# Moving the convolution, the norms, the bias and the transposes of a four-branch mixer to other engines and places

## The reference

```python
h = _rmsnorm(x, g_mix[l])
gate_pre, a_in, na_qkv, dil_qkv, swa_q, swa_kv = jnp.split(h @ w_in[l], IN_SPLITS, axis=-1)
# branch a: a * sigmoid(g), depthwise convolution of 31 taps over the rows, layernorm, silu
# branch b: norm of q and k, softmax(q k / 8 + bias[head, row, key]) v over near keys (4 heads)
# branch c: norm and rope, three dilated windows; branch d: norm and rope, window of 128, sinks
gates = jax.nn.sigmoid(gate_pre.reshape(bsz, seq, N_BRANCH, D_MODEL) + gate_b[l])
x = x + jnp.sum(gates * jnp.einsum('bsnc,ncd->bsnd', ys, w_branch[l]), axis=2) @ w_out[l]
```

## Time and profile before

| | us |
|---|---|
| runs | 1758.84 and 1754.22; median 1758.84 |
| profiled execution | 1755.16 |
| its span | 1753.5 |
| first mixer in it | about 868 to 1117 |
| second mixer in it | about 1311 to 1558 |

### The profile page before, as it was taken

How to read it: one execution, slowest core, us unless ns; L and a number is a source line. 1 busy time by engine, 2 the same in 40 slices (tenths; PEclk the granted TensorE clock), 3 DMA queues, 4 the chain that set the end, 5 groups by cost and what they waited for, 6 DMA issues and landing times. The chain is left out here.

```text
span 1753.5 us, 26990 instructions
## 1 busy us (share of the span) xinstructions
PE 1657.0 (94%) x10967; PEld 1493.6 (85%) x10967; DVE 1137.5 (65%) x1635; ACT 833.2 (48%) x1253; POOL 459.3 (26%) x529
## 2 busy tenths in 40 slices
PE   7889899999999889999999998999999999899998
PEld 6767799987786778998888998899988899889997
DVE  5885565545556755665467966677646796767763
ACT  6445454434345454444453336556534433656552
POOL 2400100002330010000137933043303694314430
PEclk9999999999989999999999999999999999999999
DMA  7422366555231134765465342666546434367651
GB/s 263 160 77 90 106 169 193 183 201 197 77 123 47 36 112 127 201 179 192 137 223 166 122 145 96 173 190 192 185 136 214 162 127 139 104 177 202 177 186 71
DMA packets 293165, 265.58 MB, mean 151 GB/s; under 512 B 18609, under 2 KB 254129, under 8 KB 293041
## 3 DMA queue, kind: packets, MB, share of 16 engines
q1 hardware_dynamic: 293040, 263.85, 48.5%
HBM read 262.78 MB, written 1.05 MB: 150 GB/s over the span
## 5 line engine op out<-in xcount | busy, mean ns | idle before, releaser
L144 DVE TENSOR_TENSOR w_lo<-w_raw,w_hi 128x2048 fp32r<-128x2048 f32 (+1 forms) x246 | 566.2, 2304 | 301.0 <-ACT w_hi L143 295.2
L143 ACT ACTIVATE w_hi<-w_raw 128x2048 fp32r<-128x2048 f32 (+1 forms) x246 | 465.1, 1894 | 227.8 <-PE bank L470 126.4
L1766 PE MATMUL bank<-h_hi,w_hi 128*128 128x256 f32 x1984 | 567.0, 286 | 2.9 <-DVE h_lo L259 1.1
L1767 PE MATMUL bank<-h_lo,w_hi 128*128 128x256 f32 x1984 | 562.4, 283 | 0.0
L1768 PE MATMUL bank<-h_hi,w_lo 128*128 128x256 f32 x1984 | 562.2, 283 | 0.0
L1766 PEld LDWEIGHTS bank<-h_hi,w_hi 128*128 128x128 f32 x1984 | 381.8, 192 | 4.6 <-issue 4.4
L1767 PEld LDWEIGHTS bank<-h_lo,w_hi 128*128 128x128 f32 x1984 | 381.9, 193 | 0.3
L1768 PEld LDWEIGHTS bank<-h_hi,w_lo 128*128 128x128 f32 x1984 | 381.7, 192 | 0.0
L397 PE MATMUL bank<-w_hi,h_hi 128*128 128x512 f32 (+2 forms) x304 | 118.6, 390 | 7.6 <-DVE h_lo L259 3.7
L399 PE MATMUL bank<-w_hi,h_lo 128*128 128x512 f32 (+2 forms) x304 | 116.8, 384 | 0.0
L398 PE MATMUL bank<-w_lo,h_hi 128*128 128x512 f32 (+2 forms) x304 | 116.7, 384 | 0.0
(11 more groups left out here) (433 smaller groups left out, 2998.2 us busy)
## 6 DMA issues: line engine op xcount, KB each, us to landing
w_raw<-in_w_in SPq DMA_DIRECT2D x48, 1024.0 KB, 5.1
w_raw<-in_ffn_w_in SPq DMA_DIRECT2D x88, 512.0 KB, 5.1
w_raw<-in_w_up SPq DMA_DIRECT2D x88, 512.0 KB, 5.2
w_raw<-in_ffn_w_out SPq DMA_DIRECT2D x22, 1024.0 KB, 4.9
w_raw<-in_w_down SPq DMA_DIRECT2D x22, 1024.0 KB, 4.9
w_raw<-in_nsa_w_in SPq DMA_DIRECT2D x10, 1024.0 KB, 5.5
...
```

The costliest lines, as they stand in the source:

```text
L143: return act.activation(hi, raw, ACT.Copy)
L144: return dve.tensor_tensor(self.lo[:, cut_slot, 0:k * n], raw, hi.bitcast(F32), ALU.subtract)
L1766: pe.matmul(out, h, hi[:, f, :], start=(f == 0), stop=False)
L1767: pe.matmul(out, h, lo[:, f, :], start=False, stop=False)
```

## The change

The convolution leaves VectorE: ScalarE makes the products of both halves (`convolve`: taps 0 to 3 in the projection, then four taps, eight instructions, in each of attention steps 0 to 6) into four buffers that lie in the part of `gates` that is written last, and GpSimd only adds, 30 sums of 128x512. Each product from tap 5 waits for the sum four taps back. The near branch's q and k become one segment of eight heads, whose gain is applied as a scale in the copy after the transposes, so its second multiplication goes. The bias is no longer a product on TensorE: it comes from DRAM in its final layout, laid out on the host, in one transfer in place of eight; VectorE multiplies it by 8 and adds the near mask once a layer, in place, and the attention reads the result as its mask. The projection's blocks come in the order window, middle, middle, near. Its last block no longer cuts a further chunk ahead of the norm (`hurry=3`). The transposes of q and k come in two parts with gate chunk 1 between them, two gate chunks precede the attention instead of three, and steps 12 and 13 have gate chunks too. Of `turn_out`, groups 0 and 1 move into step 12. Layernorm comes one step earlier. Eight of the 32 gate sigmoids (was 16) precede the branch products. In the branch products VectorE cuts the next chunk before, not after, the previous column's remainder. `...` marks what is left out.

```diff
+    def pe(self, pe, ready=None, groups=None):
+        for g, (i, tiles) in self.part(groups):
+            earlier = [n for n in range(g) if self.banks[n] == self.banks[g]]
+            if earlier:
...
+            if not self.short and j < hurry:
                 w.round_to(act, self.last[j] + 2)
...
+            if not self.short and j < hurry:
                 w.cut_to(dve, self.last[j] + 2)
...
-                          ALU.mult).then_inc(self.normed, 1)
+                          ALU.mult).then_inc(self.normed if self.segments[i][3] is not False else self.gained, 1)
+        if self.segments[i][3] is False:
+            return
...
                 for u, head in enumerate(p["heads"]):
-                    ins = pe.matmul(self.score(i, u), head["q"], head["k"], start=True, stop=head.get("bias") is None)
-                for u, head in enumerate(p["heads"]):
-                    if head.get("bias") is not None:
-                        ins = pe.matmul(self.score(i, u), self.k.flip[:, :], head["bias"], start=False, stop=True)
+                    ins = pe.matmul(self.score(i, u), head["q"], head["k"], start=True, stop=True)
...
+                        in0=self.score(i, u), in1=head["mask"] if p["mask"] is None else p["mask"],
...
-        segments = [(NA_Q, 4, HD, g(0), None, 0), (NA_Q + S, 4, HD, g(1), None, 0), (DL_Q, 4, HD, g(2), rope, 1),
-                    (DL_Q + S, 4, HD, g(3), rope, 2), (SW_Q, 4, HD, g(4), rope, 3), (SW_K, 2, HD, g(5), rope, 3)]
+        segments = [(SW_Q, 4, HD, g(4), rope, 0), (SW_K, 2, HD, g(5), rope, 0), (DL_Q, 4, HD, g(2), rope, 1),
+                    (DL_Q + S, 4, HD, g(3), rope, 2), (NA_Q, 8, HD, False, None, 3)]
...
+        tiles += [at(c + P * i) for c in (DL_Q, NA_Q, NA_Q + S, DL_Q + S) for i in range(2)]
+        turn = Turn(k, "feat", tiles, feat, banks=[4, 5, 6, 7, 4, 6],
+                    gains={3: cols[:, C2_NA:C2_NA + 1], 4: cols[:, C2_NA + 1:C2_NA + 2]})
+        turn_segment = [0, 0, None, None, 2, 2, 4, 4, 4, 4, 3, 3]
...
-        gate_banks = [0, 1] + [2, 3] * 5 + [2, 3, 3, 3]
+        mask_step, mixed_ready, biased = s("mask_step"), s("mixed_ready"), s("biased")
+
+
+        AHEAD, LN_STEP, OPEN = 2, 9, 2
+        gate_banks = [0, 1] + [2, 3] * 4 + [2] + [3] * 5
         bank_free = [(project.copied_d, 3)] * 2 + [(project.copied_d, 4)] * 2
-        bank_free += [(gated, j - 1) for j in range(4, 14)] + [(gated, 14), (gated, 15)]
-        OPEN = 4
-        AHEAD, LN_STEP = 3, 10
+        bank_free += [(gated, j - 1) for j in range(4, 12)] + [(gated, j) for j in range(12, 16)]
 
...
+                sp.dma_start(bias[:, :, :], a["rpb_2"][layer]).then_inc(bias_in, 16)
...
+
                 for tap in range(1, TAPS):
-                    weight = cols[:, C2_CONV + TAPS + tap:C2_CONV + TAPS + tap + 1]
-                    pool.wait_ge(cv_step, 2 * tap - 1)
-                    pool.tensor_scalar(tap_product[:, :], padded[:, 1, tap:tap + S], weight, None, ALU.mult)\
-                        .then_inc(cv_step, 1)
-                    pool.wait_ge(cv_step, 2 * tap)
-                    pool.tensor_tensor(conv[:, 1, :], conv[:, 1, :], tap_product[:, :], ALU.add).then_inc(cv_step, 1)
+                    pool.wait_ge(cv_tap, 2 * tap + 2)
+                    if tap > 1:
+                        pool.wait_ge(cv_sum, tap - 1)
+                    pool.tensor_tensor(conv[:, :, :], conv[:, :, :], taps[tap % 4], ALU.add).then_inc(cv_sum, 1)
...
+                def convolve(act, first, last):
+                    for tap in range(first, min(last, TAPS)):
+                        if tap >= 5:
+                            act.wait_ge(cv_sum, tap - 4)
+                        for n in range(2):
+                            weight = cols[:, C2_CONV + n * TAPS + tap:C2_CONV + n * TAPS + tap + 1]
+                            u = padded[:, n, tap:tap + S]
+                            if tap == 0:
+                                act.activation(conv[:, n, :], u, ACT.Identity, bias=cols[:, C2_CONVB + n:C2_CONVB + n + 1],
+                                               scale=weight).then_inc(cv_tap, 1)
+                            else:
+                                act.activation(taps[tap % 4][:, n, :], u, ACT.Copy, scale=weight).then_inc(cv_tap, 1)
+
...
-                project.act(act, squares)
+                    if j == 1:
+                        act.wait_ge(cols_in, 32)
+                        act.wait_ge(cv_mul, 2)
+                        convolve(act, 0, 2)
+                    if j == 2:
+                        convolve(act, 2, 4)
...
+                project.act(act, squares, hurry=3)
...
-                w.round_to(act, gate_chunks[AHEAD - 1] + 2)
+                w.round_to(act, gate_chunks[2])
                 act.wait_ge(hn.sums, len(segments))
-                turn.act(act)
+                turn.act(act, range(0, 3))
+                w.round_to(act, gate_chunks[3])
+                turn.act(act, range(3, 6))
...
-                            open_gates(act, j)
...
+                turn_out.act(act, range(0, 2))
...
+                act.wait_ge(gated, 13)
+                open_gates(act, 0)
+                w.round_to(act, mix_chunks[1])
+                open_gates(act, 1)
                 act.wait_ge(ln_lo, 1)
                 act.activation(y_hi[:, 0:2, :], conv[:, :, :], ACT.Copy).then_inc(ln_act, 1)
-                w.round_to(act, mix_chunks[0] + 2)
+                turn_out.act(act, range(2, 3))
+                w.round_to(act, mix_chunks[2])
...
+                        dve.wait_ge(bias_in, 16)
+                        table = bias[:, :, :].rearrange("p h (e c) -> p (h e) c", c=HD)
+                        dve.scalar_tensor_tensor(out=table, in0=table, scalar=8.0, in1=free(near[:, :], [[0, 24], [1, HD]]),
+                                                 op0=ALU.mult, op1=ALU.add).then_inc(biased, 1)
+
+                project.dve(dve, sums, hurry=3)
...
+                    if i == 13:
+                        turn_out.dve(dve, range(0, 2))
+                    if 1 <= i <= 13:
                         gate(dve, AHEAD + i - 1)
                     make_masks(dve, i)
-                    convolve(dve, AHEAD + i)
...
+                turn.dve(dve, range(0, 3))
                 cut(dve, 0)
-                hn.dve_scale(dve, 4)
...
+                turn.dve(dve, range(3, 6))
+                gate(dve, 1)
                 cut(dve, 1)
-                for j in range(AHEAD):
-                    gate(dve, j)
-                turn.dve(dve)
-                for j in range(1, AHEAD):
-                    cut(dve, j)
...
+                dve.wait_ge(biased, 1)
...
-                turn_out.dve(dve)
                 dve.wait_ge(ln_act, 4)
                 dve.tensor_tensor(y_lo[:, 0:2, :], conv[:, :, :], y_hi[:, 0:2, :].bitcast(F32), ALU.subtract)\
                    .then_inc(ln_lo, 1)
+                gate(dve, 15)
+                turn_out.dve(dve, range(2, 3))
 
...
+                    if j >= 3 and j % 2 == 1:
+                        w.cut_to(dve, mix_chunks[0] + j // 2 + 2)
                     if j:
                         mixed_rest(j - 1)
-                    if j >= 3 and j % 2 == 1:
...
+                    if i == 0:
+                        turn.wait_done(pe)
+                    if i == 1:
+                        pe.wait_ge(gated, 2)
                     if i == LN_STEP:
-                        pe.wait_ge(cv_tap, TAPS)
-                        pe.wait_ge(cv_step, 2 * TAPS - 1)
-                        pe.wait_ge(gated, 13)
+                        pe.wait_ge(cv_sum, TAPS - 1)
...
-                    if AHEAD + i < len(gate_chunks):
-                        gate(pe, AHEAD + i)
...
                         ins.then_inc(ln_back, 1)
+                    if i == 12:
+                        pe.wait_ge(att.stored, 4)
+                        turn_out.pe(pe, groups=range(0, 2))
+                    gate(pe, AHEAD + i)
...
-                turn_out.pe(pe)
+                turn_out.pe(pe, groups=range(2, 3))
...
+        "rpb_2": i["na_rpb_2"].reshape(2, -1)[:, near_rows],
```

170 lines of the change are left out of this document (74 added, 96 removed).

## The result

The changed kernel takes 1733.08 us (median of four: 1735.18, 1730.96, 1737.46, 1730.97) against 1754.22 for the kernel before (median of three: 1758.84, 1754.22, 1753.35; a fourth, disturbed execution of 3575 us is left out of all comparisons). The ratio is 0.9881, 95% interval [0.9862, 0.9900]: 21 us less, under 2%. The interval is 0.2% wide to either side, some 3 us, so a change far smaller than the 35 us that the prediction named can be told from none here. The forecast was 1726, range 1716 to 1739, with 0.80 on "within 2%". So the range holds and the change is within 2%; the forecast lies 7 us too low, and rival A's narrow range of 1720 to 1732 was just missed. The profiled executions give 1755.16 - 1735.18 = 20.0 us, where the sum said 29.4.

What follows compares the result with a forecast made beforehand. TensorE, busy 94% of the span, was taken to bound the kernel through its work, waits and clock. The terms 5.5 + 8.0 + 7.6 + 1.3 + 5.4 + 1.6 = 29.4 us off 1755.16 gave 1726, range 1716 to 1739.

Steps and rivals of the forecast that it cites:

- rival A: Whole kernel: the sum of terms holds as it stands, 1726 us, own range 1720 to 1732; chance 0.60.
- Bias off TensorE: Attention steps 1 to 3: without bias products each loses 0.91 us, 5.5 in all; TensorE waits 0.8 a layer at block four.
- The bias's transfers: Loading the bias: one bigger transfer replaces eight and lands long before it is needed; no gain or cost counted.
- The head: Projection's end to the first scores: a wait of 2.0 us remains, half a clock fall counted; 4.0 a layer gained, 8.0 in all.
- The attention's steps: Convolution moved to ScalarE and GpSimd during attention: TensorE does not begin to wait, steps of 7.86 us, cost 0.
- rival D: Attention and layernorm: GpSimd's sums hold the kernel from 2.3 us a sum on; 1791 us at 3.5; chance 0.04.
- The end: Output's transposes: split beside gate chunks 14 and 15, the 0.48 and 3.32 us waits go; 3.8 a layer, 7.6.
- tight, yet not over: Branch products' column loop: ScalarE's added gate sigmoids take 1.7 us a column beside 2.9 of TensorE, so they fit.
- Branch and residual waits: Branch and residual products: the cut ahead of the remainder leaves 1.2 of 3.9 us of waits; 2.7 a layer, 5.4.
- The clock's 1.3 + 1.6: First layer's end: slow clock goes, 1.3 us in the branch products and 1.6 behind the residual product's 2.04 us wait.
- C: Head: VectorE's two-input bias and norm instructions shut GpSimd out, delaying rotations and near factors; 1732 to 1738 us; chance 0.18.
- B: Head and end: GpSimd gets its instructions in between VectorE's, no waits left; 1717 us, over 2% faster; chance 0.15.

Runs made afterwards that it cites:

- before_bias: The kernel before with only the bias part: host table, one load, VectorE's instruction, no bias product; stage 493.0 us, time 1751.92 us, ratio 0.9987.
- no_sums: The changed kernel with each of GpSimd's convolution sums cut to one column; stage 473.9 us, time 1725.21 us, ratio 0.9833 to the kernel before.
- sums_wait: The changed kernel, but GpSimd starts the first convolution sum only after VectorE has scaled the near segment; stage 478.4 us, time 1730.88 us.
- bias_early: The changed kernel with VectorE's bias instruction one projection block earlier; stage 474.6 us against 479.5, time 1727.98 us.
- out_one: The changed kernel with the output's transposes and copies in one piece after the last gate chunk, as before the change; stage 481.3 us, time 1733.21 us.
- act_order: out_one with ScalarE again doing sixteen gate sigmoids ahead of layernorm's last steps, as before the change; stage 488.7 us, time 1741.66 us.
- cut_after: The changed kernel with VectorE's weight cut again behind the previous column's remainder in the branch products; stage 482.5 us, time 1735.97 us.

## Why the prediction was right, and where it was off

Measured on TensorE's timeline, both layers (a gate chunk more or less before a landmark is put at 5.84):

| part | predicted | measured | how |
|---|---|---|---|
| stage start to step 1's scores | 8.0 | 4.9 | head 2.6 + 2.9, ahead of it -0.8 + 0.2 |
| steps 1 to 4 | 5.5 | 3.5 | 33.27 and 33.33 became 31.54 twice |
| step 5 to the branch products | 7.6 | 7.4 | 3.7 twice |
| branch products, residual, clock | 8.3 | 4.6 | 3.7 in the first layer, 0.9 in the second |
| sum | 29.4 | 20.4 | |

- **What bounds it.** Right: TensorE, its waits and its clock. Every gain and loss that was located stands in one of these three. Two waits were not foreseen, the 0.70 before gate chunk 1 and the 0.71 in step 4, where the prediction had 7.86 us throughout and no wait over 0.5.
- **Bias off TensorE.** The step's 0.91 was right (7.86 for 8.77 in steps 2 and 3, 6.97 for 7.87 in step 1), and so was the instruction, 1.83 for 1.7. The wait at the fourth block, 0.93 for 0.8, was close by luck: the 0.8 takes off 0.3 for the half-width norm where the text has 0.5, with which it would be 0.6. The term was still 2.0 too high: I asked what hides the new instruction, but not what the removed products had hidden. VectorE's masks in step 3 had 8.77 us; in 7.86 they make the 0.71 (before_bias shows it without the convolution's part; in no_sums it goes with the bias products still absent, so both have a share in it).
- **The bias's transfers** were priced at nothing ("lands long before"), and there was something to gain. In the second layer of the kernel before, the eight transfers take SyncE 7.40 us to issue ahead of the weights; ScalarE waits 2.46 for a chunk, and TensorE 0.95 at a projection block. The last row is the changed kernel's one transfer.

```profile
1310.52 7.40 SPq L2311 DMA_DIRECT2D mix_bias<-in_rpb  x8
...
1330.73 1.92 ACT L143 ACTIVATE w_hi<-w_raw 128x2048 fp32r<-128x2048 f32 x1 [2.46 <-DMA w_raw<-in_w_in]
...
1335.09 0.50 PE L397 MATMUL bank<-w_hi,h_hi 128*128 128x512 f32 x1 [0.95 <-DVE w_lo L144]
...
1300.73 0.42 SPq L2310 DMA_DIRECT2D mix_bias<-in_rpb  x1
```

  No profile with the one transfer has this wait, so about 1.0 of the table's first row (its 0.2 beside the -0.8) is this and not the head. That the transfers cause it is read from one profile of the kernel before; no run changes them alone.
- **The head**, 3.1 too high, and about 4 without the gain just named. The near power was 2.90 for an estimated 2.9 and the sum 1.21 for 1.2. The largest failing term is "VectorE then scales 1024 numbers (1.2)": 2.31, since GpSimd's first sum starts 0.06 us before it (sums_wait). The rotated scaling started at 3.0 for an assumed 2.2 (at 1.5 in bias_early), so the cut that gate chunk 1 needs ended at 7.8 for 7.0, and TensorE, there at 7.2, waited 0.70. The copy came at 18.0 for 16.4 and the wait was 2.62 for 2.0. The clock fell in both layers, where I had counted half.
- **The attention's steps.** ScalarE's 6.10 of a step for 6.2, VectorE freed to 5.16. A sum took 1.80 on average where I had 1.95, so rival D was rightly at 0.04 and none of it came. But "Cost: 0" (of the convolution's move) looked only at whether the sums are in time, not at whom they hold up: that is the 0.71's other half.
- **The end.** The 7.6 were right, for the wrong reason: I gave them to the split of the transposes; out_one gives that 0.2 in the first layer, act_order gives ScalarE's order 4.4 on top. The waits went as read from the earlier trace rows, but by another of the change's edits than the one I named. I had that order in the text only as a load ("tight, yet not over").
- **Branch and residual waits.** The failing step here is the 5.4 for the cut ahead of the remainder. By the list of waits 3.9 became 2.3 a layer (0.73, 0.19, 0.83, 0.54) where I left 1.2, and in time only 1.2 a layer came (cut_after), 2.5 for 5.4: "the last two cuts come about 1 us late" stands there as two waits, 0.83 and 0.54, which with the 0.19 cost all that the 2.04 had cost. The clock's 1.3 + 1.6 came as forecast, in the first layer: the residual product to the end of the stage went from 25.1 to 23.5 us, and the six columns from 18.98 to 18.10. They are not at the 17.73 of the second layer, where no clock had fallen: 0.4 us a layer is lost that the sum did not have, in two small stops, for VectorE's last copy of the output and at the third column (out_one, without the split, takes 17.50).
- **The rivals.** A's mechanism held, with a sum 9 us off; the outcome is C's 1732 to 1738, and C's cause is part of it: of bias_early's 2.4 us a layer all but the 0.93, and the scaling's 1.1. I had held the six rotation instructions against C as undisturbed, by the earlier trace rows. That row has one line of the six. In the same trace others had met a cut:

```profile
921.10 2.37 POOL L633 TENSOR_TENSOR mix_rope_parts<-mix_proj,rope_tables 128x64 f32<-128x64 f32 x1
...
932.25 2.38 POOL L634 TENSOR_TENSOR mix_rope_parts<-mix_proj,rope_tables 128x64 f32<-128x64 f32 x1
```

  B was wrong: GpSimd does meet the cuts (2.36, 2.37, 2.25 us for an instruction of 0.32).
